# Where S5's output turns, lag products and lag matrices stand in the order of the engines

## The chip, the cores and the metric

The kernel runs on one core of one Trainium2 chip. The metric is the device time of one execution in microseconds (us); of the kernel before there are three runs, and their median is the time that counts. The profile is of one more execution.

## The reference, cut to what matters

The program computes two blocks on 512 latent tokens of 1024 channels: a block of gMLP and RWKV7, then two layers with 256 context tokens beside the latent ones, the first with MLA attention, the second with an S5 state space mixer. Only the S5 mixer is touched. Its core, per direction, group of 16 channels and chunk of tokens:

```python
def step(h, u_chunk):
    bu = jnp.einsum('btgs,gps->btgp', u_chunk.astype(jnp.complex64), b_bar)
    a = jnp.broadcast_to(lam_bar, bu.shape)
    _, xs = lax.associative_scan(_ssm_combine, (a, bu), axis=1)
    xs = xs + powers[None] * h[:, None]
    y = jnp.einsum('btgp,gsp->btgs', xs, cmat).real
    return xs[:, -1], y

y_l = d_skip * u_l + y_forward + y_backward      # both directions, latent tokens
y = gelu(y_l);  ya, yb = split(y @ w_glu + b_glu)
out = ((ya * sigmoid(yb)) * silu(g)) @ w_out
```

There are 128 groups with 64 complex states each, in two directions. All is float32.

## The kernel before, in words

**Tiles and pairs.** The 2048 channels of S5 are 16 tiles (`KE`) of 128 channels; a tile has 8 groups, taken two at a time as 4 pairs (`TILE_PAIRS`); a pair has the number n = 4m + pair. Tokens are taken in chunks of `STEP` = 8: 64 latent and 32 context chunks. For each pair:

- `turn_pe` (L2480) transposes the pair's `b_pow` into PSUM bank 2, and `turn_act` (L2491) copies it to `b_pow_t`.
- `x_pe` (L2526) multiplies it with the chunked input `u_t`, into bank 6 or 3.
- `state_dve` (L2535 to L2563) modulates, scans over the chunks (L2551, with `decay` that ACT makes for each pair at L2500) and demodulates: the chunk-start states `x_in`.
- `y_pe` makes the output in banks 5 and 7, columns 0 to 127, for two groups: two products with the lag matrix `lag_m` (L2578: what a chunk's own tokens give) and 8 products of `x_in` with `c_pow` (L2582). `y_act` (L2594) copies it to `y_tm`.

For each tile:

- `u_project_pe` (L2386) projects the tile's u two tiles ahead, in parts (`TOKENS`: three, three, two and none of eight k for pairs 0 to 3); in pair 3 `u_act` (L2401, L2403) copies it out, SP stores it to DRAM (L2415) and loads it back turned (L2424).
- `lags_pe` (L2448) makes the next tile's lag matrices in bank 4 in pair 2, `lags_dve` (L2461, L2464) copies them, SP stores them (L2894), and loads them back as `lag_m` in eight transfers (L2901).
- `y_turn_pe` (L2602) transposes the finished tile's output into bank 2 in pair 0 of the next, `y_turn_act` (L2610) applies the gelu, GpSimd stores it (L2679).
- GpSimd and ACT round the weights of u in pairs 0 and 1 (L389, L401).

**What sets the order.** Each engine runs a program of its own, in the order in which it is written, and waits on semaphores that count the steps of the others. TensorE's loop is `s5_pe`: for a pair x(n+1), in pair 0 the output turns of the tile before, the turn of n+2, in pair 2 the lag matrices, the part of u, y(n). DVE's is `s5_dve`: a state for each pair, in pair 2 followed by the copy of the lag matrices. ACT's is `s5_act`: decay of n+1, the gelu in pair 0, the b_pow copy of n+2, rounding or `u_act`, the copy of y(n). SP's order for a tile: b_pow of the next tile, lag store, store of the next tile's u, the eight lag loads, the next tile's parameters, its u loads, a weight slot.

Of the kernel before, what the change touches and what calls it, by code (L numbers as in the profile page):

```python
# [15 lines left out]
ACT = mybir.ActivationFunctionType  # L16
# [4 lines left out]
P = 128  # L21
# [3 lines left out]
T = 512  # L25
# [28 lines left out]
PAIRS = GROUPS // 2  # L54
STEP = 8
C_LAT, C_CTX = T // STEP, CTX // STEP
C_ALL = C_CTX + C_LAT
TILE_PAIRS = PAIRS // KE
# [111 lines left out]
def build(nc, io, known):  # L170
# [5 lines left out]
    with memory:  # L176
        psum = memory.enter_context(nc.psum_tensor("psum", [P, 8, BANK], F32))

        pe_done = memory.enter_context(nc.semaphore("pe_done"))
        act_done = memory.enter_context(nc.semaphore("act_done"))  # L180
# [7 lines left out]
        def at(*step):  # L188

            who, count = known.get(step, ("pe", 1))  # L190
            return done[who], count
# [18 lines left out]
        lags_moved = [memory.enter_context(nc.semaphore(f"lags_moved_{i}")) for i in range(4)]  # L210
# [14 lines left out]
        def mask(name):  # L225
            if name in CHUNK_MASKS:
                n = len(MASKS) * P + CHUNK_MASKS.index(name) * CHUNK
                return const[:, n:n + CHUNK]
            n = MASKS.index(name)
            return const[:, n * P:(n + 1) * P]  # L230
# [20 lines left out]
        def bank(n, a=0, b=BANK):  # L251
            return psum[:, n, a:b]
# [489 lines left out]
        def half(e):  # L742
            return slice(64 * e, 64 * e + 64)
# [1556 lines left out]
        s5 = ExitStack()  # L2300
# [5 lines left out]
        b_pow_t = sb(s5, "b_pow_t", [2, 4, P])  # L2306
        u_w = sb(s5, "u_w", [4, 2, HALF_SLOT])
        u_t = sb(s5, "u_t", [2, TPD, C_CTX + C_ALL])
# [4 lines left out]
        y_out = sb(s5, "y_out", [2, T])  # L2313
# [123 lines left out]
        def lags_pe(pe, m):  # L2437

            if m >= KE:
                return  # L2440
            pe.wait_ge(*ready(c_pow_ready, m))
            pe.wait_ge(*at("s5", "b_split", m))
            if m >= 1:
                pe.wait_ge(*at("s5", "lag_copy", m - 1))
            for i, (d, lo) in enumerate(((1, 1), (0, 0))):
                for ri in range(2):
                    for pair in range(TILE_PAIRS):
                        ins = nc.tensor.matmul(psum[32 * pair:32 * pair + 32, 4, 112 * i:112 * i + P],  # L2448
                                               b_bar_split[:, ri, 2 * pair + d, :, :],
                                               c_pow[:, m % 2, ri, 2 * pair + d, lo:lo + STEP, :],  # L2450
                                               start=(i == 0 and ri == 0), stop=(i == 1 and ri == 1), skip_group_check=True)
            ins.then_inc(pe_done, 1)
            pe_count.up("s5", "lag_mm", m)

        def lags_dve(dve, m):
            if m >= KE:
                return
            dve.wait_ge(*at("s5", "lag_mm", m))
            if m >= 2:
                dve.wait_ge(lags_moved[m % 2], 16 * (m // 2))  # L2460
            nc.vector.tensor_copy(lags[:, m % 2, :], bank(4, 0, 240)).then_inc(dve_done, 1)  # L2461
            dve.wait_ge(dve_done, dve_count.up("s5", "lag_copy", m))
            zero_lag = lags[:, m % 2, 112:128]
            nc.vector.scalar_tensor_tensor(out=zero_lag, in0=eye[:, :], scalar=col("s5_d", m), in1=zero_lag,  # L2464
                                           op0=ALU.mult, op1=ALU.add).then_inc(dve_done, 1)
            dve.wait_ge(dve_done, dve_count.up("s5", "lag", m))

        def turn_pe(pe, n):
            m, pair = divmod(n, TILE_PAIRS)
            if m >= KE:  # L2470
                return
            pe.wait_ge(*ready(b_pow_ready, m))
            if n >= 1:
                pe.wait_ge(*at("s5", "b_pow_t", n - 1))
            if pair == 2 and m > 0:
                pe.wait_ge(*at("s5", "yT", m - 1))
            for d in range(2):
                for ri in range(2):
                    j = 2 * d + ri
                    ins = nc.tensor.transpose(bank(2, j * P, (j + 1) * P),  # L2480
                                              b_pow[:, m % 2, ri, 2 * pair + d, :, :].rearrange("p s i -> p (s i)"), mask("ident"))
            ins.then_inc(pe_done, 1)
            pe_count.up("s5", "b_turned", n)
# [29 lines left out]
        def x_pe(pe, n):  # L2513
            if n >= PAIRS:
                return
            pe.wait_ge(*at("s5", "b_pow_t", n))
            if n % TILE_PAIRS == 0:
                m = n // TILE_PAIRS
                pe.wait_ge(u_loaded[m % 2], 16 * STEP * (m // 2 + 1))
            if n >= 2:  # L2520
                pe.wait_ge(*at("s5", "x_read", n - 2))
            for d in range(2):
                for ri in range(2):
                    j = 2 * d + ri
                    for e in range(2):
                        ins = nc.tensor.matmul(psum[half(e), X_BANK[n % 2], j * C_ALL:(j + 1) * C_ALL],  # L2526
                                               b_pow_t[:, n % 2, j, half(e)], u_seq(n, d, e), start=True, stop=True)
            ins.then_inc(pe_done, 1)
            pe_count.up("s5", "x", n)
# [38 lines left out]
        def y_pe(pe, n):  # L2568
            m, pair = divmod(n, TILE_PAIRS)
            pe.wait_ge(*at("s5", "x_in", n))  # L2570
            if n >= 1:
                pe.wait_ge(*at("s5", "y_tm", n - 1))
            if pair == 0:
                pe.wait_ge(lags_moved[2 + m % 2], 16 * 8 * (m // 2 + 1))
            cp = c_pow[:, m % 2, :, :, :, :]
            out = [psum[0:C_LAT, 5 + 2 * e, 0:P] for e in range(2)]
            for e in range(2):
                nc.tensor.matmul(out[e], u_t[:, m % 2, 2 * pair + e, C_CTX:C_ALL], lag_m[:, m % 2, 2 * pair + e, :], start=True, stop=False)  # L2578
            for d, lo in ((0, 1), (1, 0)):
                for ri in range(2):  # L2580
                    for e in range(2):
                        ins = nc.tensor.matmul(out[e], x_in[half(e), n % 2, d, ri, :], cp[half(e), ri, 2 * pair + d, lo:lo + STEP, :],  # L2582
                                               start=False, stop=(d == 1 and ri == 1))
            ins.then_inc(pe_done, 1)
            pe_count.up("s5", "y", n)

# [10 lines left out]

        def y_turn_pe(pe, m):
            pe.wait_ge(*at("s5", "y_tm", TILE_PAIRS * (m + 1) - 1))
            pe.wait_ge(*at("s5", "b_pow_t", min(TILE_PAIRS * (m + 1) + 1, PAIRS - 1)))  # L2600
            for s in range(STEP):
                ins = nc.tensor.transpose(bank(2, s * C_LAT, (s + 1) * C_LAT), y_tm[0:C_LAT, s, :], mask("ident")[0:C_LAT, 0:C_LAT])  # L2602
            ins.then_inc(pe_done, 1)
            pe_count.up("s5", "y_turned", m)

        def y_turn_act(act, m):
            act.wait_ge(*at("s5", "y_turned", m))
            if m >= 2:
                act.wait_ge(y_stored[m % 2], 16 * (m // 2))
            nc.scalar.activation(y_out[:, m % 2, :], bank(2), ACT.Gelu_apprx_tanh).then_inc(act_done, 1)  # L2610
            act.wait_ge(act_done, act_count.up("s5", "yT", m))


# [3 lines left out]
        def s5_pe(pe):  # L2617
            for k in range(KD):
                u_project_pe(pe, 0, k)
            lags_pe(pe, 0)  # L2620
            turn_pe(pe, 0)
            for k in range(KD):
                u_project_pe(pe, 1, k)
            x_pe(pe, 0)
            turn_pe(pe, 1)
            for m in range(KE):
                for pair in range(TILE_PAIRS):
                    n = m * TILE_PAIRS + pair
                    x_pe(pe, n + 1)
                    if pair == 0 and m > 0:  # L2630
                        y_turn_pe(pe, m - 1)
                    turn_pe(pe, n + 2)
                    if pair == 2:
                        lags_pe(pe, m + 1)
                    for k in TOKENS[pair]:
                        u_project_pe(pe, m + 2, k)
                    y_pe(pe, n)
            y_turn_pe(pe, KE - 1)
# [42 lines left out]
        def s5_dve(dve):  # L2681
            lags_dve(dve, 0)
            for m in range(KE):
                for pair in range(TILE_PAIRS):
                    state_dve(dve, m * TILE_PAIRS + pair)
                    if pair == 2:
                        lags_dve(dve, m + 1)

        s5.close()

# [434 lines left out]
```

## Time and profile before

| | |
|---|---|
| median of three runs | 2508.6 us (2506.0 to 2516.5) |
| the profiled execution | 2512.8 us |
| its span | 2511.1 us |
| S5 stage, about | 1503 to 1927 us of the span |
| steady tiles in it | 24.2 to 24.8 us each |
| TensorE busy | 2210.5 us, 88% of the span |
| VectorE (DVE) | 1335.3 us, 53% |
| ScalarE (ACT) | 784.7 us, 31% |
| GpSimd (POOL) | 587.0 us, 23% |
| mean granted TensorE clock | 0.955 of full speed |

Starts are in us from the start of the span. A group of instructions in a timeline is one line with the start of its first, the busy time of all, and how many there are (a float32 product counts as several). In brackets stands the engine's idle time before the group and what released it, where there was any. The time from one group's start to the next's is what the first costs the engine, since ends are modelled and overlap.

### The profile page before, as it was taken

To read this page: it belongs to the slowest core of one execution; us is meant where nothing else is said; L and a number is where in the kernel's file an instruction comes from. 1 tells how busy PE (TensorE), PEld (TensorE's weight loads), DVE (VectorE), ACT (ScalarE), POOL (GpSimd) and SP (SyncE) were. 2 spreads that over 40 slices of the span, in tenths; PEclk is the share of its full clock that TensorE was granted. 3 is DMA by queue.
4 is the path that set the end of the run, shared out by engine and by line. 5 is a ranking of instruction groups with operands and counts; after the bars stand their busy time and mean duration, and the time that the engine had idled before them with its cause. 6 is when DMAs were issued, how large, how long until landed. Compare 5 with 4: busy or idle time off the path is not lost. (4 is left out here: it accounts for less than half of the span.)

```text
span 2511.1 us, 39658 instructions
## 1 busy us (share of the span) xinstructions
PE 2210.5 (88%) x15634; PEld 1585.5 (63%) x15634; DVE 1335.3 (53%) x2356; ACT 784.7 (31%) x1430; POOL 587.0 (23%) x1099
## 2 busy tenths in 40 slices
PE   5998877679998888888889957999997999999997
PEld 4876666555554444444455536777775778888774
DVE  1266664348993444344359965777775323333344
ACT  1324532221102333333310043444443432222333
POOL 0453111210015888888001102111110000000000
PEclk8999999889999999999999978999998999999998
DMA  7321332322452111111024423778775323332220
GB/s 275 101 86 49 137 136 104 110 86 97 147 188 76 48 62 47 60 50 47 30 76 163 167 87 133 237 224 250 221 232 186 98 84 101 93 100 94 91 84 34
DMA packets 105001, 294.58 MB, mean 117 GB/s; under 512 B 12400, under 2 KB 49520, under 8 KB 96240
## 3 DMA queue, kind: packets, MB, share of 16 engines
q1 hardware_dynamic: 92464, 227.02, 27.8%
q0 software_dynamic: 12352, 65.02, 7.1%
q8 instruction: 125, 2.05, 0.3%
q14 instruction: 60, 0.49, 0.1%
HBM read 225.01 MB, written 66.98 MB: 116 GB/s over the span
## 5 line engine op out<-in xcount | busy, mean ns | idle before, releaser
L412 PE MATMUL psum<-split,w_split 128*128 128x512 f32 x1920 | 440.5, 392 | 10.1 <-DVE split L430 6.0
L412 PEld LDWEIGHTS psum<-split,w_split 128*128 128x128 f32 x1920 | 363.4, 189 | 87.2 <-DVE split L430 6.5
L394 DVE TENSOR_TENSOR w_split<-ring,w_split 128x512 fp32r<-128x512 f32 x192 | 133.0, 693 | 340.3 <-ACT w_split L389 340.0
L1836 POOL TENSOR_TENSOR h<-h 128x8 f32<-128x8 f32 (+6 forms) x672 | 276.0, 411 | 52.8
L389 ACT ACTIVATE w_split<-ring 128x512 fp32r<-128x512 f32 x192 | 121.7, 634 | 363.7 <-PE psum L412 360.4
L1617 PE MATMUL psum<-h,ring 128*128 128x256 f32 (+1 forms) x640 | 210.1, 491 | 0.9 <-DVE h L1598 0.9
L2386 PE MATMUL psum<-h,u_w 128*128 128x256 f32 (+1 forms) x768 | 151.8, 351 | 32.2 <-DVE h L2346 31.3
L1617 PEld LDWEIGHTS psum<-h,ring 128*128 128x128 f32 x640 | 123.6, 193 | 85.5 <-issue 75.4
L2260 PE MATMUL psum<-gate,ring 128*128 128x512 f32 (+1 forms) x512 | 165.4, 486 | 1.2 <-issue 1.2
L2386 PEld LDWEIGHTS psum<-h,u_w 128*128 128x128 f32 x768 | 121.4, 195 | 52.8 <-ACT h L2331 25.8
L2125 DVE TENSOR_REDUCE sm<-psum 128x1 f32<-128x768 f32 (+1 forms) x96 | 74.9, 780 | 141.6 <-PE psum L2019 139.8
L2260 PEld LDWEIGHTS psum<-gate,ring 128*128 128x128 f32 x512 | 97.2, 190 | 69.3 <-issue 62.7
L412 PE MATMUL psum<-h_split,in_w 128*128 128x512 f32 x600 | 139.2, 392 | 1.5 <-POOL in_w L401 1.5
L412 PEld LDWEIGHTS psum<-h_split,in_w 128*128 128x128 f32 x600 | 111.9, 188 | 27.6 <-ACT prev L657 2.1
L2010 PE MATMUL psum<-ckv,q_abs 128*128 128x256 f32 (+1 forms) x320 | 112.1, 492 | 14.1 <-ACT prob L2145 14.1
L401 POOL TENSOR_TENSOR u_w<-ring,u_w 128x512 fp32r<-128x512 f32 x32 | 50.5, 1578 | 314.5 <-ACT u_w L389 272.3
L401 POOL TENSOR_TENSOR in_w<-ring,in_w 128x512 fp32r<-128x512 f32 x50 | 77.4, 1548 | 137.2 <-ACT in_w L389 135.1
L2043 PE MATMUL psum<-area,ckv_tm 128*128 128x512 f32 (+1 forms) x256 | 102.6, 555 | 1.0 <-ACT area L2160 1.0
L412 PE MATMUL psum<-h,w_split 128*128 128x512 f32 x384 | 94.6, 411 | 5.3 <-DVE w_split L394 5.3
L2594 ACT ACTIVATE y_tm<-psum 64x128 f32<-64x128 f32 x128 | 34.8, 272 | 192.1 <-PE psum L2582 131.9
L412 PEld LDWEIGHTS psum<-h,w_split 128*128 128x128 f32 x384 | 75.0, 196 | 24.7 <-ACT w_split L389 5.4
L2010 PEld LDWEIGHTS psum<-ckv,q_abs 128*128 128x128 f32 x320 | 59.9, 199 | 40.2 <-ACT prob L2145 17.6
(394 smaller groups left out, 3560.2 us busy)
## 6 DMA issues: line engine op xcount, KB each, us to landing
ring<-in_s_glu SPq DMA_DIRECT2D x64, 512.0 KB, 3.5
ring<-in_w_mod SPq DMA_DIRECT2D x48, 512.0 KB, 5.3
made_c_pow<-area POOLq DMA_DIRECT2D x16, 1152.0 KB, 5.3
c_pow<-made_c_pow SPq DMA_DIRECT2D x16, 1152.0 KB, 5.5
made_b_pow<-area POOLq DMA_DIRECT2D x16, 1024.0 KB, 4.8
ring<-in_s_in SPq DMA_DIRECT2D x32, 512.0 KB, 6.7
b_pow<-made_b_pow SPq DMA_DIRECT2D x16, 1024.0 KB, 9.9
ring<-in_w_in SPq DMA_DIRECT2D x29, 512.0 KB, 3.6
```

Source lines behind the costliest of these rows:

```text
L389: nc.scalar.activation(rounded(buffer(u, 0)), source(u), ACT.Copy).then_inc(act_done, 1)
L394: nc.vector.tensor_tensor(rounded(buffer(u, 1)), source(u), buffer(u, 0), ALU.subtract).then_inc(dve_done, 1)
L401: nc.gpsimd.tensor_tensor(rounded(buffer(u, 1)), source(u), buffer(u, 0), ALU.subtract).then_inc(pool_done, 1)
L412: ins = nc.tensor.matmul(out, rounded(buffer(u, w)[:, ks]), values(x, k), start=(first and k == 0 and n == 0), stop=(last and k == UNIT_K ...
L1617: ins = nc.tensor.matmul(o, tile_w(("mla_in", m), k), h2[:, k, a:a + n], start=(k == 0), stop=(k == KD - 1))
L1836: nc.gpsimd.tensor_tensor(o, a, b, op).then_inc(pool_done, 1)
L2010: mm(o, q_abs_of(h, u), ckv[:, a:a + m], start=True, stop=False)
L2043: ins = mm(o, ckv_tm[:, k, :], pt[:, k, :], start=(k == 0), stop=(k == kt - 1))
L2125: v.tensor_reduce(sm[:, n % 3, 0:1], both(b)[:, 0:keys], AX.X, ALU.max).then_inc(dve_done, 1)
L2260: ins = nc.tensor.matmul(o, tile_w(("mla_out", 2 * m + k // KD), k % KD), gate2[:, k, a:a + n], start=(k == 0), stop=(k == KE - 1))
L2386: ins = nc.tensor.matmul(o, rounded(u_w[:, u % 4, w, kk * P:(kk + 1) * P]), h3_part(x, k)[:, a:a + size], start=(k == 0 and n == 0), stop= ...
L2594: nc.scalar.activation(y_tm[0:C_LAT, :, g * GS:(g + 1) * GS], psum[0:C_LAT, 5 + 2 * e, 0:P].rearrange("p (t i) -> p t i", i=GS), ACT.Copy) ...
```

## The change

It has three parts. (1) The output turns go to banks 5 and 7, columns 128 to 383, beside the columns of the output products, in place of bank 2; the gelu reads both halves. `turn_pe` no longer waits for the gelu; `y_pe` of pair 0 does. The output turns' own wait for the b_pow copy goes. (2) In `y_pe` the products with `x_in` come first and those with `lag_m` last, and the wait for the lag loads stands between them. (3) In pair 2 `lags_pe` stands ahead of `x_pe` and `turn_pe`, and `lags_dve` ahead of `state_dve`.

```diff
 def turn_pe(pe, n):
             if n >= 1:
                 pe.wait_ge(*at("s5", "b_pow_t", n - 1))
-            if pair == 2 and m > 0:
-                pe.wait_ge(*at("s5", "yT", m - 1))

 def y_pe(pe, n):
-            if pair == 0:
-                pe.wait_ge(lags_moved[2 + m % 2], 16 * 8 * (m // 2 + 1))
+            if pair == 0 and m > 0:
+                pe.wait_ge(*at("s5", "yT", m - 1))
             cp = c_pow[:, m % 2, :, :, :, :]
             out = [psum[0:C_LAT, 5 + 2 * e, 0:P] for e in range(2)]
-            for e in range(2):
-                nc.tensor.matmul(out[e], u_t[...], lag_m[:, m % 2, 2 * pair + e, :], start=True, stop=False)
             for d, lo in ((0, 1), (1, 0)):
                 for ri in range(2):
                     for e in range(2):
-                        ins = nc.tensor.matmul(out[e], x_in[...], cp[...], start=False, stop=(d == 1 and ri == 1))
+                        nc.tensor.matmul(out[e], x_in[...], cp[...], start=(d == 0 and ri == 0), stop=False)
+            if pair == 0:
+                pe.wait_ge(lags_moved[2 + m % 2], 16 * 8 * (m // 2 + 1))
+            for e in range(2):
+                ins = nc.tensor.matmul(out[e], u_t[...], lag_m[:, m % 2, 2 * pair + e, :], start=False, stop=True)

 def y_turn_pe(pe, m):
             pe.wait_ge(*at("s5", "y_tm", TILE_PAIRS * (m + 1) - 1))
-            pe.wait_ge(*at("s5", "b_pow_t", min(TILE_PAIRS * (m + 1) + 1, PAIRS - 1)))
             for s in range(STEP):
-                ins = nc.tensor.transpose(bank(2, s * C_LAT, (s + 1) * C_LAT), y_tm[...], mask("ident")[...])
+                a = P + (s % 4) * C_LAT
+                ins = nc.tensor.transpose(bank(5 + 2 * (s // 4), a, a + C_LAT), y_tm[...], mask("ident")[...])

 def y_turn_act(act, m):
-            nc.scalar.activation(y_out[:, m % 2, :], bank(2), ACT.Gelu_apprx_tanh)
+            nc.scalar.activation(y_out[:, m % 2, :].rearrange("p (b t) -> p b t", b=2), psum[:, 5:8:2, P:P + T // 2],
+                                 ACT.Gelu_apprx_tanh)

 def s5_pe(pe):
                     n = m * TILE_PAIRS + pair
+                    if pair == 2:
+                        lags_pe(pe, m + 1)
                     x_pe(pe, n + 1)
                     if pair == 0 and m > 0:
                         y_turn_pe(pe, m - 1)
                     turn_pe(pe, n + 2)
-                    if pair == 2:
-                        lags_pe(pe, m + 1)

 def s5_dve(dve):
-                    state_dve(dve, m * TILE_PAIRS + pair)
                     if pair == 2:
                         lags_dve(dve, m + 1)
+                    state_dve(dve, m * TILE_PAIRS + pair)
```

## Rows read from the trace of the kernel before

**Rows 1.** Windows, all engines: length, busy time and count, granted clock, DMA share, GB/s.

```profile
1655.00:1680.00 25.00, 23.09 (x265) 18.78 (x264) 18.64 (x46) 11.77 (x30) 3.87 (x3) 1.00 0.75 232
...
1886.00:1900.00 14.00, 8.98 (x92) 7.12 (x96) 7.68 (x21) 4.86 (x13) 0.54 (x1) 0.76 0.91 276
```

**Rows 2.** Chain that ended last, 1864 to 1880 us: start, length, what.

```profile
1864.07 2.55 DMA lag_m<-lags
...
1866.76 0.62 PE psum L2578 x4
1867.38 1.02 PE psum L2582 x16
1868.40 0.81 PE psum L2526 x16
1869.21 0.59 PE psum L2480 x4
1869.80 3.12 PE psum L2386 x18
...
1875.91 1.01 PE psum L2448 x32
1876.93 2.31 PE psum L2386 x12
```

**Rows 3.** Timeline of TensorE, 1654 to 1672 us: start, busy, group, idle before.

```profile
1654.85 0.88 PE L2526 MATMUL psum<-u_t,b_pow_t 128*64 128x96 f32 x16
...
1656.25 1.08 PE L2448 MATMUL psum<-c_pow,b_bar_split 128*32 128x128 f32 x32
...
1664.98 0.71 PE L2602 MATMUL psum<-const,y_tm 64*128 64x64 f32 x8
1666.53 0.63 PE L2480 MATMUL psum<-const,b_pow 128*128 128x128 f32 x4 [0.84 <-ACT y_out L2610]
...
1671.37 0.62 PE L2578 MATMUL psum<-lag_m,u_t 128*64 128x128 f32 x4 [1.07 <-DVE const L2563]
```

**Rows 4.** Timeline of DVE, 1657 to 1663 us: lag copy, then state of pair 3.

```profile
1657.45 0.41 DVE L2461 COPY const<-psum 128x240 f32<-128x240 f32 x1 [2.47 <-issue]
...
1658.16 0.56 DVE L2543 TENSOR_TENSOR s_tmp<-psum,table 128x384 f32<-128x384 f32 x1
...
1659.88 0.96 DVE L2551 TENSOR_TENSOR_SCAN s_tmp<-decay,s_tmp 128x384 f32<-128x384 f32 x1
...
1661.67 0.63 DVE L2563 TENSOR_TENSOR const<-s_tmp 128x64 f32<-128x64 f32 x4
```

**Rows 5.** Timeline of ACT and SP, 1658 to 1669 us.

```profile
1658.15 0.32 SPq L2894 DMA_DIRECT2D lags<-const  x1
...
1661.89 0.80 ACT L2500 ACTIVATE decay<-const,decay 128x190 f32<-128x190 f32 x2
...
1662.67 0.60 ACT L2491 ACTIVATE b_pow_t<-psum 128x512 f32<-128x512 f32 x1
...
1663.86 0.39 ACT L2403 ACTIVATE u_cm<-psum 128x256 f32<-128x256 f32 x1
...
1664.69 4.56 SPq L2901 DMA_DIRECT2D lag_m<-lags  x8
```

**Rows 6.** Timeline, first tile, ends of the 13 periods, tile 14, last state.

```profile
1547.64 0.62 PE L2578 MATMUL psum<-lag_m,u_t 128*64 128x128 f32 x4 [2.36 <-DMA lag_m<-lags]
...
1556.90 0.88 PE L2526 MATMUL psum<-u_t,b_pow_t 128*64 128x96 f32 x16
...
1695.32 0.62 PE L2578 MATMUL psum<-lag_m,u_t 128*64 128x128 f32 x4 [0.80 <-DMA lag_m<-lags]
...
1874.45 0.88 PE L2526 MATMUL psum<-u_t,b_pow_t 128*64 128x96 f32 x16
...
1891.65 1.09 PE L2578 MATMUL psum<-lag_m,u_t 128*64 128x128 f32 x4 [4.89 <-DMA lag_m<-lags]
...
1922.22 0.63 DVE L2563 TENSOR_TENSOR const<-s_tmp 128x64 f32<-128x64 f32 x4
```

More of the change, by code:

```diff
@@ L2572, in y_pe @@
                 pe.wait_ge(*at("s5", "y_tm", n - 1))
-            if pair == 0:
-                pe.wait_ge(lags_moved[2 + m % 2], 16 * 8 * (m // 2 + 1))
+            if pair == 0 and m > 0:
+                pe.wait_ge(*at("s5", "yT", m - 1))
             cp = c_pow[:, m % 2, :, :, :, :]
             out = [psum[0:C_LAT, 5 + 2 * e, 0:P] for e in range(2)]
-            for e in range(2):
-                nc.tensor.matmul(out[e], u_t[:, m % 2, 2 * pair + e, C_CTX:C_ALL], lag_m[:, m % 2, 2 * pair + e, :], start=True, stop=False)
             for d, lo in ((0, 1), (1, 0)):
@@ L2581, in y_pe @@
                     for e in range(2):
-                        ins = nc.tensor.matmul(out[e], x_in[half(e), n % 2, d, ri, :], cp[half(e), ri, 2 * pair + d, lo:lo + STEP, :],
-                                               start=False, stop=(d == 1 and ri == 1))
+                        nc.tensor.matmul(out[e], x_in[half(e), n % 2, d, ri, :], cp[half(e), ri, 2 * pair + d, lo:lo + STEP, :],
+                                         start=(d == 0 and ri == 0), stop=False)
+            if pair == 0:
+                pe.wait_ge(lags_moved[2 + m % 2], 16 * 8 * (m // 2 + 1))
+            for e in range(2):
+                ins = nc.tensor.matmul(out[e], u_t[:, m % 2, 2 * pair + e, C_CTX:C_ALL], lag_m[:, m % 2, 2 * pair + e, :], start=False, stop=True)
             ins.then_inc(pe_done, 1)
@@ L2599, in y_turn_pe @@
             pe.wait_ge(*at("s5", "y_tm", TILE_PAIRS * (m + 1) - 1))
-            pe.wait_ge(*at("s5", "b_pow_t", min(TILE_PAIRS * (m + 1) + 1, PAIRS - 1)))
             for s in range(STEP):
-                ins = nc.tensor.transpose(bank(2, s * C_LAT, (s + 1) * C_LAT), y_tm[0:C_LAT, s, :], mask("ident")[0:C_LAT, 0:C_LAT])
+                a = P + (s % 4) * C_LAT
+                ins = nc.tensor.transpose(bank(5 + 2 * (s // 4), a, a + C_LAT), y_tm[0:C_LAT, s, :], mask("ident")[0:C_LAT, 0:C_LAT])
             ins.then_inc(pe_done, 1)
@@ L2609, in y_turn_act @@
                 act.wait_ge(y_stored[m % 2], 16 * (m // 2))
-            nc.scalar.activation(y_out[:, m % 2, :], bank(2), ACT.Gelu_apprx_tanh).then_inc(act_done, 1)
+            nc.scalar.activation(y_out[:, m % 2, :].rearrange("p (b t) -> p b t", b=2), psum[:, 5:8:2, P:P + T // 2],
+                                 ACT.Gelu_apprx_tanh).then_inc(act_done, 1)
             act.wait_ge(act_done, act_count.up("s5", "yT", m))
```

## The prediction

> **What bounds the kernel now.** I read the table of the page first, then the chain that ended last, then the timeline of one S5 tile on all engines, then the clock by windows. Only the S5 stage (about 1503 to 1927 us) is touched. It is 16 tiles of four pairs; call the pairs 0 to 3, y(k) the output products of pair k (L2578 and L2582), x(k) its input products (L2526), state(k) its DVE work. In the chain, a tile goes from y(0) through TensorE's program to the end of the tile, then over one ACT copy into SP's eight lag loads, and from the last load's landing back to the next y(0) [rows 2]. TensorE runs at full clock throughout (1.00 in the window) [rows 1], yet is idle twice in a tile: 0.84 us ahead of the turn of b_pow (L2480), released by the gelu, and 1.07 us ahead of y(0) [rows 3].
>
> The second idle is the one that counts. The profile names the DVE as its releaser, but state(3) ends at 1662.30 and a state takes 4.14 us (1658.16 to 1662.30), so state(0) was over at about 1666.5, 4.9 us before y(0) at 1671.37 [rows 3, 4]. What came last were the lag loads: u_act's second copy ends at 1664.25, the loads start at 1664.69 behind the store of u [rows 5], and y(0) starts 7.12 us after that copy [rows 3]. The lag *store*, which the change hastens, was issued at 1658.15, six us earlier: SP then sat waiting for u [rows 5].
>
> This closes a cycle that I can test. TensorE's pieces from the chain: y is 0.58 + 1.02 = 1.60 us, x 0.81, turn with 18 products of u 0.59 + 3.12 = 3.71, turn alone 0.59, lag matrices (L2448) 1.01, 12 products of u 2.31 [rows 2]. From y(0)'s start to the output turns (L2602) that is 1.60 + (0.81 + 3.71 + 1.60) + (0.81 + 0.59 + 1.01 + 2.31 + 1.60) + (0.81 + 0.59 + 1.60) + 0.81 = 17.85 us. The mean period is (1874.45 - 1556.90) / 13 = 24.43 us [rows 6]; so output turns to y(0) take 6.58 us in the mean (6.39 in the tile shown [rows 3]). The output turns start 0.73 us after u_act's end [rows 3, 5], so the leg from u_act's end to y(0) is 7.31 us in the mean.
>
> **The change, part by part.** *Output turns in banks 5 and 7, gelu no longer awaited by L2480.* This removes the 0.84 us before L2480, 15 times. But TensorE only reaches y(0) earlier, where the lag loads are last: worth nothing by itself. Nothing is queued earlier on SP by it, because u_act belongs to pair 3, before the output turns. The new wait of y(0) for the gelu, and of all queued behind it, is covered by the 3.12 us of u products [rows 2], against 0.6 us of activation. The gelu reads two half banks instead of one; at most some tenths of a us on ACT, which is idle there. Cost 0.
>
> *Lag products last.* The 16 x_in products (1.02 us) of y(0) need only x_in and c_pow; they now run while the loads land, and only 0.58 us is left behind the landing [rows 2]. Worth 1.02 us a tile as long as the loads are last. In pairs 1 to 3 the order is neutral, 1.60 us either way.
>
> *Lag matrices first in pair 2, on TensorE and DVE.* TensorE does the same work. On DVE the copy of the lag matrices now stands *ahead* of state(2), and it can't start before L2448 is done, which follows y(1). In the kernel before, state(2) was over early and DVE then sat idle 2.47 us until the copy [rows 4]; after, state(2) waits for the copy, and all behind it does too: state(3), state(0), and through their scans ACT's decay, the b_pow copy and u_act. Take time 0 at the end of y(1). L2448 starts at 0; the copy starts 1.20 later (1656.25 to 1657.45) [rows 3, 4]; state(2) 0.71 later (1657.45 to 1658.16), at 1.91, and ends at 6.05 [rows 4]. TensorE meanwhile does L2448, x(3), a turn and 12 products of u, 1.01 + 0.81 + 0.59 + 2.31 = 4.72 [rows 2], and so waits at y(2) for about 1.4 us, till 6.11. y(2), x(0'), turn end at 9.11. state(3) follows state(2), 6.09 to 10.23: y(3) waits 1.2 us, till 10.29. u_act comes behind the decay, which waits for state(3)'s scan: that ends 2.68 after its state's start (1658.16 to 1660.84) [rows 4], at 8.77; decay starts at 8.87, the b_pow copy 0.78 later, u_act's end 1.58 after that (1661.89, 1662.67, 1664.25) [rows 5]: 11.23. In the kernel before, y(1)'s end to u_act's end is 1654.85 to 1664.25, 9.40 [rows 3, 5]. So the loads start **1.83 us later in each tile**. The DMA path as such is unchanged; b_pow and parameter loads keep their order and gain slack.
>
> *Sum of a period.* 11.23 + 7.31 = 18.54 for the landing; TensorE is there after y(3) (ends 11.89), x, output turns 0.57, turn and u 3.71 and the 1.02 of products: 18.00, so the loads are still last, by half a us. Then 0.58, and pair 1 with 0.81 + 3.71 + 1.60 = 6.12: **25.24 us against 24.43, +0.81** (which is 1.83 - 1.02). Thirteen periods: +10.5 us.
>
> *Head.* y(0) of tile 0 starts at 1547.64 after 2.36 us of idle for the loads, and y(1) ends at 1556.90 [rows 6]. After: landing at 1547.64, then 0.58 + 6.12 gives 1554.34, -2.6; but parts of that stretch ran at the lower clock, so between -1.0 (the 1.02 us alone) and -2.6. I take -2.2, since the idle before the lag products is halved.
>
> *Tail.* From y(1) of tile 13 (1874.45) to the end of the last state (1922.22 + 0.63 = 1922.85) is 48.40 [rows 6]. After: the landing leg at y(0) of tile 14 is no shorter, 18.5 to 19.0, y(1) ends at 22.1 to 22.6, then copy and six states in a row instead of five: 1.20 + 0.71 + 6 x 4.18 = 27.0. That is 49.1 to 49.6, +0.7 to +1.2 at full clock. Before, the granted clock fell to 0.76 in 1886 to 1900 after a wait of 4.89 us [rows 1, 6]; a wait of 3 us remains, and dearer products behind it can add up to 1.3. I take +1.5. The stage ends as before, since the last output group is the same work.
>
> Total +10.5 - 2.2 + 1.5 = **+9.8 us**. The profiled execution took 2512.8 us (span 2511.1 and 1.7 around it), the median is 2508.6, 4.2 less; the sum is a difference between stretches and carries over: 2522.6 for the profiled run, **2518.4** for the median.
>
> Bounds of the term that decides. The leg of 7.31 varies: the tile at 1695.32 has an idle of 0.80 instead of 1.07 [rows 3, 6], a leg of 6.85. If all were so, TensorE would be last at 18.00 and the period 24.70: +3.5 in thirteen. As far above the mean, 7.77: period 25.70, +16.5. With head and tail: **+1 to +18, so 2510 to 2527**. The Trainium skill (DMA: Bandwidth & Descriptors, Anatomy of one DMA) gives a transfer a fixed cost of about 2.0 us that is mostly completion; the trace agrees with 2.55 us from the last lag load's issue to its landing [rows 2], and by the page's figure, as an estimate, only 0.5 us of the leg could vanish, which would end at the same lower bound.
>
> **Rivals.** *A, the clock falls* (chance 0.15). After, TensorE idles 1.4 and 1.2 us with only 3.0 us of work between, then again 0.5 us; before it idles 0.84 and 1.07 with 3.7 between, and keeps 1.00 [rows 1, 3]. Against it: single idles of that size left the clock alone. For it: in tile 14 the lag products after the 4.89 us idle took 1.09 instead of 0.62 [rows 2, 6], half clock. If it falls each time at y(2) or y(3), y, x and turn (3.0 us) cost up to 3.0 more, of which the 0.5 us of waiting absorbs a part and of which a part is after the cycle's way into ACT: about +1.5 us a tile, +20, in all +30: 2538. The Trainium skill (TensorE: Matmul & The Clock Gate, A second HAM failure mode) says that short idles between groups of products can make the clock swing although no single one is long, which speaks for this rival; no row of the steady tiles shows it.
>
> *B, the gain stands* (0.06). If DVE's 2.47 us of idle ahead of the copy [rows 4] could hold the moved copy, state(2) would be ready when TensorE comes (4.72), and the period would be 24.43 - 1.02 = 23.41: -13.3, with the head -2.2 about -16: 2493. This needs state(2) to start by 0.5, and its point is the copy's start, which L2448 holds at 1.20. So the idle is no cover, it was the wait for that very product. The reading is left a small chance for a shorter way through DVE or ACT that I don't see.
>
> *C, the loads shrink* (0.14). Part of the loads' issue time stands in the first load, directly behind u's store (4.56 us for eight [rows 5]). With the lag store further off and less traffic beside it, the leg could drop below 6.8; then TensorE is last, period 24.70, and the total is +2.8: 2511.
>
> **Chances and range.** Main case 0.65, 2518, own range 2510 to 2527. About 0.5% or 12.5 us is what a measurement can tell from no change. Of the main case a third lies above +12.5 us: with A, slower is 0.36; faster is B, with a little for scatter of the median, 0.06; the rest, 0.58, within 0.5%. The range takes in C and most of the main case and not A and B, with 2 us of scatter: 2506 to 2529.
>
> **What would show it.** Right: an idle of about 1.4 us ahead of y(2) and 1.2 ahead of y(3), released by the DVE, in every tile; the DVE idle before the copy longer than 2.5 us, and none between state(2), state(3) and state(0); no idle ahead of L2480; about 0.5 us between the x_in products and the lag products of y(0); a period of 25.2. Wrong: no idle at y(2) (B), a period under 24.8 with no idle before the lag products (C), x or y of 1.5 us and more in steady tiles or a granted clock below 1.00 (A).

## The result, and the profile after

Change: **2519.3 us** in the median of 16 runs (2514.3 to 2524.6), beside 2511.8 (2505.0 to 2518.3) for the kernel before in its 16 runs on the same chip. The ratio is **1.0034, 95% interval 1.0022 to 1.0045**: 7.5 us longer, within 0.5%. The forecast was +9.8 us, and 2518.4.

The profiled execution took 2521.1 us. The first lines of its page, span and busy time of each engine:

```profile
span 2519.3 us, 39641 instructions
...
PE 2199.9 (87%) x15634; PEld 1584.7 (63%) x15634; DVE 1323.0 (53%) x2356; ACT 782.5 (31%) x1430; POOL 579.8 (23%) x1099
```

Three windows of its S5 stage (columns as in [rows 1]): the head, the 13 steady tiles, and part of tiles 14 and 15.

```profile
1547.00:1557.00 10.00, 9.25 (x124) 7.65 (x121) 3.46 (x12) 3.92 (x10) 1.28 (x1) 1.00 0.69 212
1557.00:1885.00 328.00, 285.25 (x3238) 237.51 (x3237) 231.31 (x603) 142.70 (x350) 39.80 (x37) 1.00 0.73 223
1900.00:1920.00 20.00, 15.47 (x186) 12.74 (x188) 12.78 (x36) 8.59 (x23) 0.00 (x0) 0.83 0.74 229
```

The granted clock is 1.00 (2.4 GHz) through all steady tiles and falls only behind. One steady tile on TensorE (start, busy, group, idle before and its releaser), in the place of [rows 3]. The x_in products of y are now L2578 and stand first, its lag products are L2583, x is L2524 and the turn L2478:

```profile
1604.36 1.08 PE L2448 MATMUL psum<-c_pow,b_bar_split 128*32 128x128 f32 x32
...
1610.47 1.09 PE L2578 MATMUL psum<-c_pow,const 64*64 64x128 f32 x16 [1.55 <-DVE const L2561]
...
1614.64 1.09 PE L2578 MATMUL psum<-c_pow,const 64*64 64x128 f32 x16 [1.25 <-DVE const L2561]
...
1616.97 0.71 PE L2602 MATMUL psum<-const,y_tm 64*128 64x64 f32 x8
1617.62 0.66 PE L2478 MATMUL psum<-const,b_pow 128*128 128x128 f32 x4
...
1621.34 1.09 PE L2578 MATMUL psum<-c_pow,const 64*64 64x128 f32 x16
1622.61 0.54 PE L2583 MATMUL psum<-lag_m,u_t 128*64 128x128 f32 x3 [0.19 <-DMA lag_m<-lags]
1622.89 0.30 PE L2524 MATMUL psum<-u_t,b_pow_t 128*64 128x96 f32 x1
1622.99 0.27 PE L2583 MATMUL psum<-lag_m,u_t 128*64 128x128 f32 x1
1623.02 0.90 PE L2524 MATMUL psum<-u_t,b_pow_t 128*64 128x96 f32 x15
1623.86 0.65 PE L2478 MATMUL psum<-const,b_pow 128*128 128x128 f32 x4
...
1629.18 1.08 PE L2448 MATMUL psum<-c_pow,b_bar_split 128*32 128x128 f32 x32
```

All the idles forecast are there: 1.55 us ahead of y(2) and 1.25 ahead of y(3), released by the DVE, a short one ahead of the lag products (0.19 to 0.87 in eleven of the 13 tiles, none in two), and none ahead of the turn, where [rows 3] had 0.84. The DVE in the same tile (for [rows 4]): copy of the lag matrices, first and last step of state(2), first step and scan of state(3):

```profile
1605.56 0.41 DVE L2461 COPY const<-psum 128x240 f32<-128x240 f32 x1 [6.41 <-issue]
...
1606.27 0.56 DVE L2541 TENSOR_TENSOR s_tmp<-psum,table 128x384 f32<-128x384 f32 x1
...
1609.78 0.63 DVE L2561 TENSOR_TENSOR const<-s_tmp 128x64 f32<-128x64 f32 x4
1610.45 0.56 DVE L2541 TENSOR_TENSOR s_tmp<-psum,table 128x384 f32<-128x384 f32 x1
...
1612.16 0.96 DVE L2549 TENSOR_TENSOR_SCAN s_tmp<-decay,s_tmp 128x384 f32<-128x384 f32 x1
```

Here the DVE waits 6.41 us instead of 2.47 and then runs without a gap. ACT and SP in that tile (for [rows 5]): decay, the b_pow copy, u_act's second copy, the lag loads.

```profile
1613.22 0.80 ACT L2498 ACTIVATE decay<-const,decay 128x190 f32<-128x190 f32 x2 [0.47 <-DVE s_tmp L2549]
1613.92 0.58 ACT L2489 ACTIVATE b_pow_t<-psum 128x512 f32<-128x512 f32 x1
...
1615.09 0.38 ACT L2403 ACTIVATE u_cm<-psum 128x256 f32<-128x256 f32 x1
...
1615.91 4.65 SPq L2902 DMA_DIRECT2D lag_m<-lags  x8
```

The head and the tail on TensorE, and the last state on the DVE (for [rows 6]):

```profile
1548.36 0.54 PE L2583 MATMUL psum<-lag_m,u_t 128*64 128x128 f32 x3 [0.75 <-DMA lag_m<-lags]
...
1554.91 1.08 PE L2448 MATMUL psum<-c_pow,b_bar_split 128*32 128x128 f32 x32
...
1881.13 1.08 PE L2448 MATMUL psum<-c_pow,b_bar_split 128*32 128x128 f32 x32
...
1900.45 0.54 PE L2583 MATMUL psum<-lag_m,u_t 128*64 128x128 f32 x3 [3.76 <-DMA lag_m<-lags]
1911.55 1.97 PE L2578 MATMUL psum<-c_pow,const 64*64 64x128 f32 x16 [3.63 <-DVE const L2561]
...
1931.73 0.63 DVE L2561 TENSOR_TENSOR const<-s_tmp 128x64 f32<-128x64 f32 x4
```

**Where the time went.** The stage, from the first rounding of u's weights to the first product of the gates, grew from 434.6 to 440.9 us, +6.3:

| stretch | before | after | difference |
|---|---|---|---|
| stage start to x(1) of tile 0 | 42.94 | 42.08 | -0.9 |
| x(1) to the end of y(1), tile 0 | 16.22 | 12.91 | -3.3 |
| 13 periods | 317.55 | 326.22 | +8.7 |
| end of y(1) of tile 13 to the last state's end | 48.40 | 51.23 | +2.8 |
| last state to the gates | 9.49 | 8.44 | -1.1 |

The other 2 us between the spans (2511.1 and 2519.3) lie ahead of the stage, in code that the change does not touch: the forecast was of the stage alone, and its +9.8 stands beside +6.3.

A period can be cut into three legs, and the experiments are read with them: from L2448's start to the end of u_act; from there to y(0)'s lag products; from those to the next L2448. The second leg holds the loads. Means in us:

| kernel | L2448 to u_act | to lag products | to L2448 | period |
|---|---|---|---|---|
| before | 8.00 | 7.33 | 9.10 | 24.43 |
| change | 11.14 | 7.40 | 6.55 | 25.09 |
| parts 1 and 2 | 7.87 | 7.20 | 7.80 | 22.88 |
| part 3 alone | 11.22 | 8.19 | 7.70 | 27.11 |
| parts 1 and 2, lag last in pair 0 only | 8.00 | 7.28 | 7.95 | 23.23 |
| parts 1 and 2, L2448 early on TensorE alone | 9.06 | 7.20 | 6.55 | 22.81 |

(The change, part 3 alone and the TensorE-only kernel start L2448 ahead of x and turn, which moves these from the third leg to the first: 7.80 to 6.55 or 9.10 to 7.70 in the third.)

### The profile page after: what moved, and what is told of

Read it like the earlier page. It is cut to its first block, busy times and chain, and to the rows that moved or that the text cites. A ratio compares the mean times of both kernels' runs of the same rounds, so it can differ in the third digit from the quotient of the medians.

```text
span 2519.3 us, 39641 instructions
## 1 busy us (share of the span) xinstructions
PE 2199.9 (87%) x15634; PEld 1584.7 (63%) x15634; DVE 1323.0 (53%) x2356; ACT 782.5 (31%) x1430; POOL 579.8 (23%) x1099
## 4 chain that ended last, share of the span: by engine, by line
PE 75%; DVE 10%; ACT 6%; issue 4%; DMA 3%; SPq 2%; POOL 0%; ACTq 0%; DVEq 0%; POOLq 0%
PE psum L412 28%; PE psum L1617 8%; PE psum L2260 7%; PE psum L2010 4%; PE psum L2043 4%; PE psum L2019 2%; PE psum L2386 2%; SPq L2902 2%; PE psum L322 2%; PE psum L970 2%; PE psum L2084 2%; PE psum L2077 2%; DMA lag_m<-lags 1%; DVE s_tmp L2533 1%; DVE s_tmp L2549 1%
## 5 line engine op out<-in xcount | busy, mean ns | idle before, releaser
L401 POOL TENSOR_TENSOR u_w<-ring,u_w 128x512 fp32r<-128x512 f32 x32 | 43.7, 1364 | 323.4 <-ACT u_w L389 282.8
L2578 PE MATMUL psum<-c_pow,const 64*64 64x128 f32 x1024 | 71.1, 279 | 49.8 <-DVE const L2561 49.8
L2578 PEld LDWEIGHTS psum<-c_pow,const 64*64 64x64 f32 x1024 | 55.5, 135 | 66.3 <-DVE const L2561 59.1
```

The lines of the kernel that those rows point to most:

```text
L401: nc.gpsimd.tensor_tensor(rounded(buffer(u, 1)), source(u), buffer(u, 0), ALU.subtract).then_inc(pool_done, 1)
```

## The experiments

Part 1 is the output turns in banks 5 and 7, part 2 the lag products last, part 3 L2448 and its copy ahead in pair 2. Each kernel's median and ratio are against the kernel before on the same chip (medians 2512.5, 2511.4, 2510.9 and 2512.1 in the four groups), five rounds each. Line numbers shift by a few between kernels.

**Parts 1 and 2, without part 3.** From the change:

```
-                    if pair == 2:
-                        lags_pe(pe, m + 1)
                     x_pe(pe, n + 1)
 ...
                     turn_pe(pe, n + 2)
+                    if pair == 2:
+                        lags_pe(pe, m + 1)
 ...
-                    if pair == 2:
-                        lags_dve(dve, m + 1)
                     state_dve(dve, m * TILE_PAIRS + pair)
+                    if pair == 2:
+                        lags_dve(dve, m + 1)
```

> Parts 1 and 2 of the change, without part 3 (lag matrices back behind the turn on TensorE, their copy back behind state(2) on DVE). Theory (the moved copy costs 1.83 us a tile, the lag products' new place gives 1.02, the loads of lag_m are last either way): period 24.43 - 1.02 = 23.4 us, thirteen of them -13.3, the first tile about -3: 2492 to 2498 against 2511 of before, ratio 0.993 to 0.995; no idle ahead of the products of pairs 2 and 3, about 1.3 us ahead of the lag products of pair 0. Rival (parts 1 and 2 cost the time, by the shared banks or by ACT's longer queue, and part 3 does not): as slow as the changed kernel, period near 25.

Measured 2484.3 us, ratio 0.9888 (0.9871 to 0.9905): 28 us faster than before, 35 faster than the change, and 8 below the range expected. One tile of it on TensorE:

```profile
1600.49 1.08 PE L2448 MATMUL psum<-c_pow,b_bar_split 128*32 128x128 f32 x32
...
1613.33 1.09 PE L2578 MATMUL psum<-c_pow,const 64*64 64x128 f32 x16
...
1615.55 0.54 PE L2583 MATMUL psum<-lag_m,u_t 128*64 128x128 f32 x3 [1.13 <-DMA lag_m<-lags]
...
1623.35 1.08 PE L2448 MATMUL psum<-c_pow,b_bar_split 128*32 128x128 f32 x32
```

The loads are still last (1.13 us), as forecast, but the period is 22.88 and not 23.4. The rows of the change show where 0.14 us a group (y's products and the x behind them) comes from: x's first product (1622.89) starts ahead of the last lag product (1622.99), and from the first lag product to the turn behind x it is 1.25 us (1622.61 to 1623.86), where y's 0.58 and x's 0.81 made 1.39 [rows 2]. Two such groups lie in the third leg (9.10 - 1.02 - 0.28 = 7.80) and one in the first (8.00 - 0.13 = 7.87).

**Part 1 alone.** From the kernel before, only the hunks of banks and waits (the gelu's reading of two banks goes with them):

```
-            if pair == 2 and m > 0:
-                pe.wait_ge(*at("s5", "yT", m - 1))
 ...
+            if pair == 0 and m > 0:
+                pe.wait_ge(*at("s5", "yT", m - 1))
 ...
-                ins = nc.tensor.transpose(bank(2, s * C_LAT, (s + 1) * C_LAT), ...
+                ins = nc.tensor.transpose(bank(5 + 2 * (s // 4), a, a + C_LAT), ...
```

> Part 1 alone: output turns in banks 5 and 7, no wait for the gelu at the b_pow turns. Theory (the loads of lag_m are last, so TensorE only comes earlier to the same wait): within 2 us of before, period 24.4, idle ahead of pair 0's products 0.9 us longer, about 2.1. Rival (the idle of 0.84 us ahead of the turns was time that counts): 15 x 0.84 = 12.6 us less, period 23.6, ratio 0.995.

Measured 2516.5 us, 1.0015 (1.0006 to 1.0024), 4 us above its reference, where within 2 us was expected: worth nothing, as forecast, and a little less than nothing. Its lines, and a window of 50 us:

```profile
1622.94 0.62 PE L2578 MATMUL psum<-lag_m,u_t 128*64 128x128 f32 x4 [2.35 <-DVE const L2561]
1623.49 1.54 PE L2582 MATMUL psum<-c_pow,const 64*64 64x128 f32 x16
1624.96 1.55 PE L2524 MATMUL psum<-u_t,b_pow_t 128*64 128x96 f32 x16
...
1600.00:1650.00 50.00, 45.38 (x488) 37.04 (x490) 37.51 (x92) 22.17 (x54) 7.06 (x6) 0.97 0.72 223
```

The 0.84 us ahead of the turn has joined the 1.07 ahead of y(0) and makes one idle of 1.8 to 2.6 us. In four of the 13 tiles y and x behind it then run at 1.2 GHz (1.54 and 1.55 us instead of 1.09 and 0.88), and that period takes 26.0 instead of 24.4: 6 us in all, enough for the loss. This is rival A's mechanism, in a place where I did not look for it. That the joined idle is what lowers the clock is argued from the kernel before, which has the two idles apart and keeps 1.00; the longest one here (2.64) did not lower it.

**Part 2 alone.** The hunk of y_pe, without part 1's wait. 

> Part 2 alone: the 16 x_in products ahead of the lag products. Theory: they hide behind the loads' landing, period 23.4, about -13 in the periods and -2 to -3 in the first tile, ratio 0.993 to 0.995, the same as with part 1 beside it within 2 us, since TensorE is at the lag wait 0.3 us before the landing even with the wait for the gelu. Rival (the wait only moves, because the releaser named in the profile, DVE, is the true one, x_in comes last): no change.

Measured 2489.7 us, 0.9912 (0.9896 to 0.9927), better than expected by the same overlap, but not within 2 us of parts 1 and 2. The idle for the gelu (1.09) returns ahead of L2480, the one ahead of the lag products shrinks to 0.15 to 0.65, and the period is 23.2: 0.33 more than with part 1. So beside part 2 the third of a microsecond of part 1 counts, 5 us in the medians (2489.7 to 2484.3; the two intervals overlap, the legs are the firmer evidence): with the gelu's idle TensorE comes to the lag products so late that in five of the 13 tiles it is last, and the mean leg is 7.54 instead of 7.20. One of the five is the first tile (8.57), where ACT loads a table ahead of its first gelu (1.28 us) and TensorE waits 2.54 us for it.

**Part 3 alone.** The two hunks of part 3 on the kernel before. 

> Part 3 alone: lag matrices and their copy first in pair 2. Theory: state(2) and all behind it 1.83 us later in each tile, period 24.43 + 1.83 = 26.3, +24 us and 1 to 3 in the last tiles: 2534 to 2539, ratio 1.009 to 1.011, idle of 1.5 and 1.25 us ahead of pairs 2 and 3. Rival (the lower clock after more idle is what costs): granted clock below 1.00 in the steady tiles. Rival (DVE's idle covers the moved copy): no change.

Measured 2548.3 us, 1.0146 (1.0124 to 1.0168), 9 us above the range expected. One tile:

```profile
1604.07 0.65 PE L2578 MATMUL psum<-lag_m,u_t 128*64 128x128 f32 x4 [1.10 <-DVE const L2563]
...
1608.25 0.63 PE L2480 MATMUL psum<-const,b_pow 128*128 128x128 f32 x4 [1.05 <-ACT y_out L2610]
...
1612.86 0.62 PE L2578 MATMUL psum<-lag_m,u_t 128*64 128x128 f32 x4 [0.87 <-DMA lag_m<-lags]
```

L2448 to u_act is 11.11 in most tiles, as in the change. The extra is in the leg of the loads: 8.19 instead of 7.33, of which 0.5 is issue (5.2 us for eight loads, 4.7 before). What lengthens it I can't say. The clock is 0.99 over 290 us of steady tiles and accounts for little: two tiles are long (28.82, the first, with 2.48 us of waiting for the gelu and work at half clock behind, and 27.92), and the other eleven still take 26.9 where 26.3 was expected. The parts add up: -28 and +36 make +8, the change measured +7.5.

**Part 3 in halves**, each on parts 1 and 2: L2448 early on TensorE with the copy behind state(2), and the copy ahead of state(2) with TensorE's old order (the two halves of the first diff above). 

> The changed kernel with the copy of the lag matrices back behind state(2) on DVE; L2448 stays ahead of x(3) on TensorE. Theory (all of part 3's cost is DVE's order): as the kernel without part 3, whose median was 2484, or up to 3 us more, since y(1) is then followed by L2448 and not by x; no idle ahead of the products of pairs 2 and 3. Rival (TensorE's order costs, by x(3) coming a us later to state(3)): 2495 or more and idle ahead of pair 3.

> The changed kernel with TensorE's order of before in pair 2 (x, turn, then L2448), but the copy still ahead of state(2) on DVE. Theory: the copy now waits for x, turn and L2448, 1.4 us more than in the changed kernel, so idle ahead of pair 2 about 3.0 us, period 26.3 to 26.5, 16 to 20 us above the changed kernel: 2535 to 2540. Rival (the cost is of TensorE's part): at or below the changed kernel's 2519.

TensorE's half: 2484.9 us, 0.9898 (0.9884 to 0.9911), the same as without it (2484.3); period 22.81. The DVE's half: 2549.7, 1.0153 (1.0139 to 1.0167). So all of part 3's cost is the copy's place on the DVE, and L2448 early on TensorE softens it. In the second kernel:

```profile
1614.63 1.41 PE L2578 MATMUL psum<-c_pow,const 64*64 64x128 f32 x16 [2.73 <-DVE const L2561]
...
1616.67 1.70 PE L2524 MATMUL psum<-u_t,b_pow_t 128*64 128x96 f32 x15
...
1560.00:1860.00 300.00, 257.55 (x2744) 215.00 (x2744) 195.64 (x508) 122.88 (x298) 36.23 (x33) 0.94 0.67 208
```

The DVE releases y(2) 2.73 us late, and in eleven of the 13 tiles some of the work behind runs at half clock (x of 1.5 to 1.7 us where 0.90 is usual): L2448 to u_act is 11.1 in the two others and 12.10 in the mean. That is 13 us in all, and why it is 10 us above what I expected.

**The lag loads ahead of the store of u.** To see whether the loads are really last, they are issued as soon as the lag store has landed, in four settings: parts 1 and 2, the whole change, part 2 alone, and parts 1 and 2 with L2448 early on TensorE:

```
                     sp.dma_start(io["lags"][tile % 2]..., lags[:, tile % 2, :]).then_inc(lags_moved[tile % 2], 16)
-                    if tile + 1 < KE:
-                        u_store_sync(sp, tile + 1)
                     sp.wait_ge(lags_moved[tile % 2], 16 * (tile // 2 + 1))
 ...
                                      ).then_inc(lags_moved[2 + tile % 2], 16)
+                    if tile + 1 < KE:
+                        u_store_sync(sp, tile + 1)
```

Parts 1 and 2: 

> Parts 1 and 2, and on SP the eight loads of lag_m ahead of the store of u, which so far they stand behind. Theory (the loads wait for u_act only because of SP's order): they start when the lag store has landed, about 1 us sooner, the idle ahead of pair 0's lag products goes from 1.1 to under 0.3 and TensorE sets the period, 22.0 to 22.2: 8 to 12 us below the 2484 of parts 1 and 2. Rival (the loads are bound by their own path, or the u loads, now 1 to 4 us later, come last): no gain, the idle ahead of the lag products as it was or a new one ahead of x(0).

Measured 2477.0 us, 0.9863 (0.985 to 0.9877), 7 below the same kernel with the old order, a little less than the 8 to 12 expected. The first three tiles take 21.67 us with no idle at all on TensorE, the later ones 22.36 in the middle (22.15 to 22.68) with 0.4 to 0.95 ahead of the lag products. SP shows why: b_pow's load, the lag store, the lag loads:

```profile
1665.23 0.44 SPq L2842 DMA_DIRECT2D b_pow<-made_b_pow  x1
1669.16 0.32 SPq L2895 DMA_DIRECT2D lags<-const  x1
1675.25 4.49 SPq L2900 DMA_DIRECT2D lag_m<-lags  x8
```

The loads wait 6.1 us for the store of 120 KB, issued 3.9 behind a load of 1 MB. In the tile at 1580.91, with 6.0 us between the two, it was 3.5. That the large load is what holds the small store up is a reading of these distances; no run takes the load away.

The whole change: 

> The whole change with the same order on SP (lag loads ahead of the store of u). Theory: the loads land before TensorE comes, their idle of 0.5 us goes, but the 1.55 and 1.25 us ahead of pairs 2 and 3 stay, period 24.5 to 24.7: 2510 to 2514, so part 3 costs about 2.7 us a tile here, 35 us in all. Rival (part 3's cost is only that it delays the loads): with the loads freed it costs nothing, 2475 as parts 1 and 2.

Measured 2506.8 us, 0.9982 (0.9973 to 0.9991). No idle for the loads is left, the idles of 1.54 and 1.25 ahead of y(2) and y(3) stay, and every period but one (24.88) is 24.53 (21.67 and the two idles make 24.46). The time is 3 us below the 2510 to 2514 expected. Against 2477.0 without part 3, that part costs 30 us (35 expected) though the loads have all the room they want: late loads are not what makes it dear.

Part 2 alone: 

> Part 2 and the lag loads ahead of the store of u, without part 1 (TensorE's turns still wait for the gelu). Theory (part 1 is worth nothing only as long as the loads are last; with 0.6 us of idle left for them, part 1 gives what the stall of 1.1 us exceeds that): 0.4 to 0.6 us a tile above parts 1 and 2 with the same SP order (2477), 2483 to 2486. Rival (part 1 never counts): 2477.

Measured 2483.9 us, 0.9888 (0.9871 to 0.9904), as expected. Its tiles take 22.78 us (the first 25.68), and the idle in them that the kernel with part 1 does not have is the gelu's:

```profile
1637.31 0.63 PE L2480 MATMUL psum<-const,b_pow 128*128 128x128 f32 x4 [1.08 <-ACT y_out L2610]
```

So part 1, worth nothing on the kernel before, is worth 7 us here (2483.9 to 2477.0). Some 3 of the 7 lie in the first tile, where the gelu's wait is 2.53 us for the table load and the work behind runs at half clock.

Parts 1 and 2 with L2448 early on TensorE: 

> Parts 1 and 2, L2448 ahead of x(3) on TensorE as in the change, its copy behind state(2) on DVE as before, and the lag loads ahead of the store of u. Theory (TensorE's half of part 3 is free, and brings the lag store 1.4 us sooner where DVE is idle anyway; the loads start when it has landed): the 0.6 us of idle left ahead of the lag products goes, TensorE sets the period, 21.7 to 21.8 against 22.4: 2467 to 2472. Rival (the lag store lands behind b_pow's load in the queue, whenever it is issued): 2477 as without it.

Measured **2473.6 us, 0.9851 (0.9836 to 0.9866)**, the lowest median of all, though its interval overlaps that of 0.9863 above, and 2 us above the range expected. Five periods are 21.61 us, then 21.9 to 22.9 with 0.3 to 1.2 of idle for the loads; in those the loads start 7.4 to 8.5 us behind the store's issue, so the rival named ahead of the run holds in part.

**Lag products last in pair 0 only**, on parts 1 and 2: in pairs 1 to 3 they stand first again (`start` and `stop` set to match). 

> Parts 1 and 2, but the lag products last in pair 0 only; in pairs 1 to 3 they are first as before. Theory (each output group that ends with the lag products and is followed by x is 0.14 us shorter, as the first x product starts among them): L2448 to u_act's end 8.0 instead of 7.87, y(0) to L2448 0.14 longer, period 23.1 to 23.2 instead of 22.9, 3 to 6 us above the 2484 of parts 1 and 2. Rival (the extra gain of part 2 beyond 1.02 us is the DMA leg's scatter): 2484.

Measured 2487.9 us, 0.9906 (0.9891 to 0.9921), 3.6 above parts 1 and 2. Period 23.23, and the legs say it to a hundredth: the first is 8.00 again, and the third 7.95 where 9.10 - 1.02 - 0.14 makes 7.94. The 0.14 us a group are real, and a matter of which products stand next to each other:

```profile
1603.81 0.65 PE L2578 MATMUL psum<-lag_m,u_t 128*64 128x128 f32 x4
1604.39 1.09 PE L2586 MATMUL psum<-c_pow,const 64*64 64x128 f32 x16
1605.41 0.88 PE L2524 MATMUL psum<-u_t,b_pow_t 128*64 128x96 f32 x16
1606.22 0.66 PE L2478 MATMUL psum<-const,b_pow 128*128 128x128 f32 x4
```

Here y, its lag products first, and x take 1.60 + 0.81 = 2.41 us up to the turn. What makes the overlap is not shown, and two readings fit. One is that all four lag products write one half of the columns (64 rows of the output) while every second x product goes to the other. The Trainium skill (TensorEngine Tiling (Array Packing), Key Properties) says that different tiles can load weights and multiply in parallel; by that rule, the trace agrees in that x's first product starts ahead of the last lag product. The other is the shape of the weights. Their loads (PEld) pause 0.17 us where the shape changes, as from y to x in this kernel (first line), and not where lag products and x have the same 128x64, as in the change (second line):

```profile
1605.41 0.69 PEld L2524 LDWEIGHTS psum<-u_t,b_pow_t 128*64 128x64 f32 x16 [0.17 <-issue]
...
1622.89 0.85 PEld L2524 LDWEIGHTS psum<-u_t,b_pow_t 128*64 128x64 f32 x16
```

The turn saves as much where no half is free: ahead of u's products, of its own 128x128, it costs 0.41 us (1617.62 to 1618.03 in the change), ahead of lag products 0.59 (1606.22 to 1606.81 in this kernel). No run takes the two readings apart.

**The lag store on POOL's queue**, on the fastest kernel: tiles 2 to 15 are stored by POOL, behind the y store, with semaphores of their own.

```
+        def lags_store(queue, tile):
+            queue.wait_ge(*at("s5", "lag", tile))
+            queue.dma_start(io["lags"][tile % 2]..., lags[:, tile % 2, :]).then_inc(lags_stored(tile)[0], 16)
 ...
             pool.dma_start(io["y"][m], y_out[:, m % 2, :]).then_inc(y_stored[m % 2], 16)
+            if m + 2 < KE:
+                lags_store(pool, m + 2)
```

> Parts 1 and 2, L2448 early on TensorE alone, SP's lag loads ahead of the store of u, and now also the lag store of tiles 2 to 15 issued by POOL (its own queue, which carries only the y stores here) instead of SP. In the kernel without this last edit the first six tiles take TensorE's 21.61 us; later b_pow's load of 1 MB is issued 2.3 to 3.2 us ahead of the lag store instead of 4.7, the store lands 7.4 us after its issue instead of 3.9, and the tiles take 22.5. Theory 1, the store stands behind b_pow's packets in SP's own queue: on POOL's queue it lands within 4 us in every tile, all periods are 21.6 and the time is 6 to 10 us lower, 2464 to 2468. Theory 2, the 16 DMA engines are shared and b_pow's packets hold them whichever queue the store comes from (the y store of 256 KB on POOL's queue takes 8.0 us in the median): the store lands after 6 to 8 us as before or later, and the time stays at 2472 to 2480. I lean to theory 2, 0.6 to 0.4.

Measured 2474.8 us, 0.9859 (0.9835 to 0.9883): no gain, as the second of the two theories had it. b_pow's load on SP, then the y store and the lag store on POOL, then SP's lag loads:

```profile
1658.72 0.43 SPq L2852 DMA_DIRECT2D b_pow<-made_b_pow  x1
...
1659.22 0.56 POOL L2688 DMA_DIRECT2D y_tiles<-y_out  x1 [0.30 <-POOL u_w L402]
1661.92 0.54 POOL L2684 DMA_DIRECT2D lags<-const  x1 [2.14 <-DVE const L2465]
...
1669.11 4.25 SPq L2910 DMA_DIRECT2D lag_m<-lags  x8
```

7.2 us from the store's issue to the loads, where SP's own queue took 7.4 in the same tile. The Trainium skill (DMA: Bandwidth & Descriptors, Issuing engines are not separate DMA queues) says that transfers of SP and GpSimd run on the same 16 DMA engines and interleave; the trace agrees as far as the change of queue brought nothing. Whether b_pow's load or the y store of 256 KB, which here stands ahead on POOL's own queue, holds the store up, this kernel does not tell apart.

## Why the prediction was right, and where it was not

**The path through the DVE** is the step on which the forecast rested, and it held to a few hundredths. From L2448's start: copy at 1.20 (forecast 1.20), state(2) at 1.91 (1.91), y(2) at 6.11 (6.11), y(3) at 10.28 (10.29), scan of state(3) done at 8.76 (8.77), u_act's end at 11.11 (11.23; the b_pow copy came 0.70 behind the decay and not 0.78). The idles of 1.55 and 1.25 us were forecast as 1.4 and 1.2. TensorE's x_in products of y(0) ended at 18.00, as forecast.

**The leg of the loads** was taken at 7.31 and was 7.40 in the mean; none of its bounds was needed. Single tiles ran from 6.89 to 7.82, and in the two shortest TensorE came last. Rival C (the loads shrink) fell: they did not. The Trainium skill's fixed cost of a transfer (DMA: Bandwidth & Descriptors, Anatomy of one DMA), which the prediction set beside the bounds, was measured there for transfers that GpSimd issues, and the lag loads are SP's; the range did not use it.

**The period** was forecast as 25.24 and was 25.09, +0.67 instead of +0.81. With the leg of u_act (-0.09 in the mean, 11.14) and that of the loads (+0.09), the step that failed is the sentence "In pairs 1 to 3 the order is neutral": lag products last let the work behind x begin 0.14 us sooner, and this is the rest (6.70 forecast for the third leg, 0.58 + 6.12; 6.55 measured). The kernel with the order turned in pair 0 only shows it by itself.

**Head and tail** were both mis-sized, against each other. The head gave -3.3 instead of -2.2. Of this, -2.7 lies behind the landing (9.26 before, 6.55 now, 1548.36 to 1554.91), the forecast's figure at full speed: the clock was 1.00 there, where the kernel before had 0.83 in the same ten microseconds. The other -0.6 is a landing that came sooner behind x(1), which the forecast had at nothing. The tail cost +2.8 instead of +1.5. The landing in tile 14 came 19.3 us behind y(1) of tile 13 (18.5 to 19.0 forecast), and from it to the end of y(1) it was 4.98 and not 3.6, at half clock behind the wait of 3.76; the six states in a row took 26.9 (27.0). So the later wait of 3.63, though long, is not on the path. Head and tail together, -0.5, are close to the -0.7 forecast.

**That the sum was so near is partly luck.** The stage grew by 6.3 and not 9.8; -2.0 of the difference are the first and last stretch of the table above, which the forecast had at nothing, and some 2 us outside the stage brought the whole back to +7.5 in the medians and +8.2 between the two profiles. By the forecast's own terms parts 1 and 2 bring 16 us (rival B's number) and part 3 costs 26; measured were 28 and 35 or 36. In 13 periods the first brought 20.2 (1.56 a tile: 1.02 of the forecast, 0.28 and 0.13 of overlap, 0.13 of a shorter leg), the head 3.3, the tail 2.1 and the way from the last state to the gates 1.1; the rest of the 28 lies behind the stage. The tail, from L2448 of tile 13 to the last state's end, is 44.93 us there and 47.00 before: in tile 14, too, only the lag products are left behind the landing, and its copy and state(2) come 1.1 us sooner behind it. The forecast had this at nothing for rival B. Part 3 cost 2.21 a period: y(1)'s end to u_act is 9.13 without it and 11.14 with it, and the leg 0.20 longer. The overlaps of pairs 1 and 2 that shorten the way to u_act are lost in the change, where the DVE sets that way. So of the 0.54 a tile that I missed in parts 1 and 2, part 3 takes back 0.38.

**Part 1 at nothing** was right for part 1 alone and for the stated reason, the loads being last. But I costed it on the kernel before and not beside part 2, where it brings some 5 us; with the loads early it brings 7. What I did not see is that removing a short idle ahead of a longer one makes one long idle, which went with a lower clock in four of 13 tiles.

**Rival A** did not come true in the steady tiles: two idles of 1.55 and 1.25 us with 3 us of work between left the clock at 1.00. **Rival B** fell by the row of the copy, which starts at 1.20 behind L2448; the DVE's idle was the wait for it, and it grew from 2.47 to 6.41 instead of covering anything.

Open are the leg of 8.19 in part 3 alone, what of two readings makes the overlap of 0.14 us, and what holds the lag store up.

## What to carry to other kernels

When an operation is moved ahead of a queue's other work, look up what ends the idle time in front of it: an idle that is the wait for its own input is no room for it, and everything behind it in the queue starts later (here 2.0 us a tile, all from one copy on the DVE, none from its matmuls on TensorE). Put work that needs the late operand last in its group, which was worth 0.9% here, and take away the wait that ends last before those that end earlier. A small gain by a sum of large terms of either sign should be tried part by part: two of the three parts made a kernel 1.1% faster than before, and with the lag loads ahead of the store 1.4 to 1.5%.

## What the runs showed of the hardware that I had not expected

- The first product of a group can start ahead of the last product of the group in front of it: 0.14 us where x follows lag products, gone where they stand apart. Both have weights of 128x64; between groups of different shapes the weight loads pause 0.17 us.
- Two idles of TensorE a tile, of 1.25 and 1.55 us, left the granted clock at 1.00. With one of 1.8 to 2.6 us it was 0.97 over two tiles (four of 13 tiles 1.6 us longer), with one of 2.7 and one of up to 1.4 it was 0.94 (eleven of 13 tiles longer).
- From the issue of a store of 120 KB to the loads that wait for it passed 1.7 to 4.2 us where a load of 1 MB had been issued 6.0 us earlier (parts 1 and 2 and part 2 alone, loads early), and 6.4 to 8.5 where that was 2.3 to 3.3 us earlier (TensorE's half, loads early). With the store on POOL's queue it was 6.3 to 7.6 at 2.7 to 3.6 us.
